# Eight modulation pages of layer 0 moved from between the projection pages into the feed-forward

## The chip, the cores and the metric

The kernel is one program on one core of one Trainium2 chip. The metric is device time in microseconds (us) of one execution, first as the median of several runs of the same kernel. The core has five engines that the text names: TensorE (PE: matmuls, and PEld its weight loads), VectorE (DVE), ScalarE (ACT), GpSimd (POOL) and SyncE (SP), which here only issues the transfers of weights. Sixteen DMA engines carry all transfers.

## What is computed

The reference is one inference step of a decoder with two layers, over 256 prompt tokens and 8 sample tokens (264 columns in the kernel), with a model width of 1024, all in float32. Cut to what matters here, a layer is:

```
mod = silu(c) @ w_ada_l + b_ada_l                 # 9 rows of c; w_ada_l is 1024 x 6144
sh1, sc1, gt1, sh2, sc2, gt2 = split(mod, 6)      # 1024 columns each
h = rms_norm(x, g_mix_l) * (1 + sc1) + sh1
q, k, v, u, g = in_proj(h, w_in_l, ...)           # 1024 x 4096
... attention, pooling, two branch projections, output projection ...
x = x + gt1 * (merged @ w_out_l)
h2 = rms_norm(x, g_ffn_l) * (1 + sc2) + sh2
f = swiglu(h2, ...)   in layer 0,   moe_swiglu(h2, ...)   in layer 1
x = x + gt2 * f
```

So `gt2`, the last sixth of the modulation, is needed only after the feed-forward of its layer.

## The kernel before

**Pages.** All weights of layer 0, and those of layer 1 up to its experts, are one list of pages, `stream`, written out by `layer_pages(l)`. A page is 512 KB and fills one of the 18 slots (`RING`) of the tile `ring`, page n in slot n % 18. SP walks through the list: before it loads page n it waits until page n - 18 is used (`s.pages_used`). TensorE takes the pages in the same order (`page()`) and waits for each one's arrival. Pages of the kinds in `PAIRED` come two in one transfer of 1 MB. Before the first page of `cache_v` SP reads sixteen table entries into registers. After the straight part of the list, layer 1's experts stream through the same slots and a few more.

**Modulation.** `w_ada` of a layer has 48 pages, eight for each sixth of `mod`; page n holds 128 input rows of one sixth. `modulation(l, n, b)` (L989) issues four weight loads of 32 columns and four matmuls of 256 columns for a page, and sums eight pages in one half of PSUM bank `b`. `read_mod` on DVE waits for the last page, transposes the bank (L1591) and adds the bias into `mod` (L1592). Layer 0's pages 0 to 15 come ahead of everything. Its pages 16 to 47 lie between the 32 projection pages: `later_ada(l, i)` puts four of them behind each odd projection page i from 1 to 15. Pages 32 to 47 sum into bank 1.

**Projection.** `z(i)` (L1080) is one projection page: eight matmuls of 128 x 264. Behind z(12) come the transposes of the samples' queries and keys (L1161, L1164). DVE copies them (`read_samples`, L1655 to L1661), POOL writes them to memory (`q_rows`, L685) and reads the first four back spread over all partitions (L687, 1 MB), and DVE starts the sample scores on them (`past_scores`, L1669 and L1672), two samples' worth before `comb_m` (L1793) and this layer's third `read_mod`. Meanwhile DVE forms the pooling input behind z(13) and z(14) (`window_sums`, L1687 to L1690, `pooled_minus_own`, L1697 to L1702). Behind z(17), TensorE transposes half of the values into bank 1 (`by_tokens`, L1085), and for that it waits until the third `read_mod` of the layer has read that bank (`s.mod_out`). Layer 1 has the same order, but in it no modulation page lies behind z(5), and its third `read_mod` reads eight pages instead of sixteen.

**Feed-forward of layer 0.** Before it TensorE works off sixteen modulation pages of layer 1 into bank 7 while the norm is computed. Then come four groups of hidden tiles, `FF_GROUPS = (6, 6, 5, 5)`. A group of n is n pairs of gate and up pages (`gate_up`, `column`, L981) and n down pages (`full_down`, L1277), which are freed only at the end of the group. DVE reads layer 1's modulation out of bank 7 when it begins group 1 (groups count from 0), and `add_f` uses `mod[40:48]` after the last group.

**Experts of layer 1.** 32 turns, each of gate and up pages (L1408) and down pages (L1428), some 11 MB a turn, one behind the other to the end.

Of the kernel before, what the change touches and what calls it, by code (L numbers as in the profile page):

```python
# [25 lines left out]
S = 256  # L26
# [26 lines left out]
FF_GROUPS = (6, 6, 5, 5)  # L53
# [83 lines left out]
def build(nc, A, O, const_in):  # L137
    ctx = ExitStack()
    with ctx:
        def sb(name, shape, dt=F32):  # L140
            return ctx.enter_context(nc.sbuf_tensor(name, shape, dt))

        def sem(name):
            return ctx.enter_context(nc.semaphore(name))
# [8 lines left out]
        sq = sb("sq", [P, DC, T])  # L153
# [128 lines left out]
        s = namedtuple("Semaphores", names)(*[sem(name) for name in names])  # L282
# [17 lines left out]
        def cols(w, j, n=1):  # L300

            return w[:, j * P:(j + n) * P].rearrange("(c p) n -> p c n", p=P)

        def ada_page(l, n):

            q, r = n // DC, n % DC
            return ("ada", l, n), A["w_ada"][l, r * P:(r + 1) * P, q * D:(q + 1) * D].rearrange("p (c n) -> p c n", c=DC)

        def later_ada(l, i):

            first, last = ((16, 48), (32, 40))[l]
            return range(first + 2 * (i - 1), min(first + 2 * (i + 1), last)) if i % 2 else range(0)

        def layer_pages(l):

            if l == 0:
                for n in range(16):
                    yield ada_page(l, n)
            else:
                for n in range(16, 32):  # L320
                    yield ada_page(l, n)
            for i in range(0, ZC + GC, 2):
                yield ("z", l, i), cols(A["w_in"][l], Z_ORDER[i], 2)
                yield ("z", l, i + 1), None
                for n in later_ada(l, i + 1):
                    yield ada_page(l, n)
                if i + 1 in V_AT:
                    for b in range(4):
                        yield ("v", l, 4 * V_AT.index(i + 1) + b), None
            for kind, w in (("branch", A["w_branch"]), ("out", A["w_out"])):  # L330
                for j in range(0, 8, 2):
                    yield (kind, l, j), cols(w[l], j, 2)
                    yield (kind, l, j + 1), None
            if l:
                for n in range(40, 48):
                    yield ada_page(l, n)
            if l == 0:
                for n in range(16):
                    yield ada_page(1, n)
                at = 0  # L340
                for n in FF_GROUPS:
                    for j in range(at, at + n):
                        yield ("gate", l, j), cols(A["w_ff_gate"][0], j)
                        yield ("up", l, j), cols(A["w_ff_up"][0], j)
                    for j in range(at, at + n):
                        yield ("down", l, j), A["w_ff_down"][0][j * P:(j + 1) * P, :].rearrange("p (c n) -> p c n", c=DC)
                    at += n

        stream = [page for l in range(LAYERS) for page in layer_pages(l)]
# [5 lines left out]
        for n, (key, _) in enumerate(stream):  # L355
            first = n - key[2] % 2 if key[0] in PAIRED else n
# [11 lines left out]
        def used_up(kind, l, i):  # L368

            return number[(kind, l, i)] + 1  # L370
# [591 lines left out]
        def _(pe):  # L962
            used = [0]

            def page(kind, l, i):

                n = used[0]
                assert stream[n][0] == (kind, l, i)
                at, count = arrives[n]
                pe.wait_ge(page_in[at], count)  # L970
                used[0] += 1
                if kind in PAIRED:
                    return pair_cols(at)[:, :, (i % 2) * P:(i % 2 + 1) * P]
                return slot(n % RING)
# [78 lines left out]
            for l in range(LAYERS):  # L1053
# [94 lines left out]
                for i in range(16):  # L1148
# [3 lines left out]
                    if 2 <= i < 10:  # L1152
                        j = i - 2
# [107 lines left out]
                def gate_up(c, k):  # L1261

                    for half, kind, read in ((0, "gate", s.silu_out), (1, "up", s.act_out)):
                        if c >= 2 or k:
                            pe.wait_ge(read, k + max(c - 1, 0))
                        column(bank[2 * half + c % 2][:, 0:T], page(kind, l, k + c), hT, 2 * DC * l + DC if k + c == 0 else None)

                def full_down(n, k, adds):

                    downs = [page("down", l, k + c) for c in range(n)]  # L1270
                    for j in range(DC):
                        if j >= 3 or adds:
                            pe.wait_ge(s.y_added, adds + max(j - 2, 0))
                        for c in range(n):
                            if j == 0:
                                pe.wait_ge(s.act_out, k + (c + 1))
                            mm = pe.matmul(bank[4 + j % 3][:, 0:T], downs[c][:, j, :], FFN["act"][:, c, :],  # L1277
                                           start=(c == 0), stop=(c == n - 1))
                            if j == DC - 1:
                                mm.then_inc(s.pages_used, 1)  # L1280
                        if j < DC - 1:
                            mm.then_inc(s.y_mm, 1)

                if l == 0:
                    k = 0
                    for i, n in enumerate(FF_GROUPS):
                        for c in range(n):
                            gate_up(c, k)
                        full_down(n, k, DC * i)
                        k += n  # L1290


# [173 lines left out]
            with pe.Else():  # L1466
# [8 lines left out]
                with pe.Fori(0, E) as e:  # L1475
                    with pe.Fori(0, BODIES) as b:
                        n = e * BODIES + b
                        for c in range(BODY):
                            if c >= 2:
                                pe.wait_ge(s.act_e, n * BODY + (c - 1))  # L1480
                            for r in range(DC):
                                at = eslot[2 * r]
# [13 lines left out]
                        for j in range(DC):  # L1496
                            if j >= 4:
                                pe.wait_ge(s.all_added, n * DC + (j - 3))
                            for i in range(BODY):
                                at = eslot[2 * DC + i]  # L1500
# [20 lines left out]
        def _(dve):  # L1521
            step = Step(dve, s.dve_step)
# [65 lines left out]
            def read_mod(l, b, first, last, spare, n=16):  # L1588
                at = S * (first // 8 % 2) if n == 8 else 0
                dve.wait_ge(s.pages_used, used_up("ada", l, last))  # L1590
                step(dve.transpose(spare, bank[b][:, at:at + 32 * n]))  # L1591
                return dve.tensor_tensor(mod[:, first:first + n, :], spare.rearrange("p (c n) -> p c n", c=n)[:, :, 0:NC],  # L1592
                                         vecT[:, 48 * l + first:48 * l + first + n].unsqueeze(2).broadcast_to([P, n, NC]),
                                         ALU.add)
# [10 lines left out]
            for l in range(LAYERS):  # L1605
# [159 lines left out]
                spare = ATT["prob"].rearrange("p a b -> p (a b)")[:, 0:512]  # L1765
# [22 lines left out]
                if l == 0:  # L1788
                    dve.wait_ge(s.lam_exp, 1)
                    for n in range(LAYERS):  # L1790
# [1 line left out]
                        step(dve.tensor_scalar(neglam[:, n:n + 1], neglam[:, n:n + 1], -LAM_INIT[n], None, ALU.add))  # L1792
                step(dve.scalar_tensor_tensor(out=comb_m[:, :], in0=const("comb_b", 64), scalar=neglam[0:64, l:l + 1],  # L1793
                                              in1=const("comb_a", 64), op0=ALU.mult, op1=ALU.add))
                if l:
                    read_mod(l, 1, 32, 39, spare[:, 0:S], 8).then_inc(s.mod_out, 1)
                else:
                    read_mod(l, 1, 32, 47, spare).then_inc(s.mod_out, 1)
                past_scores(2); read_v(0); past_scores(3); read_v(1); past_scores(4); past_scores(5); read_new()
                scores(0); past_scores(6); scores(1); weights(0); past_scores(7); scores(2); weights(1); scores(3); weights(2)  # L1800
                sample_top()
# [17 lines left out]
                for half in range(2):  # L1819
                    at = 520 * half  # L1820
# [53 lines left out]
                if l == 0:  # L1874
                    step(dve.memset(f, 0.0))
                    k = 0
                    for i, n in enumerate(FF_GROUPS):
                        if i == 1:
                            read_mod(1, 7, 0, 15, sq[:, :, :].rearrange("p a b -> p (a b)")[:, 0:512]).then_inc(s.mod_out, 1)
                        for c in range(n):  # L1880
                            dve.wait_ge(s.silu_out, k + c + 1)
                            dve.wait_ge(s.pages_used, used_up("up", 0, k + c))
                            dve.tensor_tensor(act_t[:, c, :], bank[2 + c % 2][:, 0:T], silu[:, c, :],  # L1883
                                              ALU.mult).then_inc(s.act_out, 1)
                        k += n
                        for j in range(DC):
                            if j < DC - 1:
                                dve.wait_ge(s.y_mm, (DC - 1) * i + j + 1)
                            else:
                                dve.wait_ge(s.pages_used, used_up("down", 0, k - 1))  # L1890
                            if i:
                                dve.wait_ge(s.y_added, DC * (i - 1) + j + 1)
                            dve.tensor_tensor(f[:, j, :], bank[4 + j % 3][:, 0:T], f[:, j, :], ALU.add).then_inc(s.y_added, 1)
                    dve.wait_ge(s.y_added, DC * len(FF_GROUPS))
                    add_f(f)
                else:
                    experts(dve, step, f, act_t, silu, add_f, read_mod)
# [26 lines left out]
```

## Time and profile before

| | us |
|---|---|
| median of 3 runs | 1658.96 |
| lowest and highest | 1658.45, 1659.12 |
| the profiled execution's own time | 1660.19 |
| its span, first to last instruction | 1658.5 |
| TensorE busy in the span | 1604.6 (97%) |
| DMA, mean of the span | 323 GB/s |

The rows further down are from that one profiled execution. "Busy" is the time in which an engine had an instruction in work; matmuls overlap, so neighbouring rows of TensorE overlap by some tenths of a microsecond. The text in square brackets at the end of a row of the timeline is the engine's idle time before that row and what ended it. Queue q1 is SP's, q0 is POOL's.

### The profile page before, as it was taken

What the parts mean: (1) busy time and instruction counts of PE and PEld (TensorE: products, weight loads), DVE (VectorE), ACT (ScalarE), POOL (GpSimd) and SP (SyncE); (2) the same over time, 40 slices, a digit from 0 to 9 for tenths busy, and PEclk for the clock granted to TensorE, in tenths of its full rate; (3) what the DMA queues carried; (4) which work ended last, traced back from release to release, by engine and by line L of the source; (5) the groups of instructions that cost most, each with busy time, mean ns of one, the idle gap of its engine ahead of it and who ended that gap; (6) DMA issues with size and microseconds to landing.
All of it is one profiled execution on the core that took longest, in us unless ns stands there. A gap on an engine that the chain in (4) does not pass through costs nothing.

```text
span 1658.5 us, 35090 instructions
## 1 busy us (share of the span) xinstructions
PE 1604.6 (97%) x15752; PEld 1016.4 (61%) x15752; DVE 423.6 (26%) x970; ACT 158.5 (10%) x410; POOL 67.3 (4%) x114
## 2 busy tenths in 40 slices
PE   6999999999999999999999999999999999999997
PEld 3778887888886888863444444654454535554444
DVE  3468353101103793542010101010101001010114
ACT  2102301000002113130000000000000000000000
POOL 3101300000000010001000000000000000000100
PEclk9999999999999999999999999999999999999999
DMA  9998868664448876439999999999999999999994
GB/s 346 386 375 301 308 214 257 162 203 147 133 140 305 269 256 216 137 134 376 402 410 399 409 409 400 408 407 398 405 395 406 404 393 402 408 390 407 409 399 187
DMA packets 225642, 535.43 MB, mean 323 GB/s; under 512 B 17069, under 2 KB 117083, under 8 KB 212690
## 3 DMA queue, kind: packets, MB, share of 16 engines
q1 hardware_dynamic: 210000, 497.11, 80.5%
q0 software_dynamic: 8608, 28.65, 4.7%
q10 hardware_dynamic: 6882, 7.38, 1.4%
q8 instruction: 127, 2.08, 0.5%
q14 instruction: 25, 0.20, 0.0%
HBM read 517.71 MB, written 15.82 MB: 322 GB/s over the span
## 4 chain that ended last, share of the span: by engine, by line
PE 79%; DMA 12%; DVE 4%; SPq 3%; issue 1%; ACT 0%; DVEq 0%
PE bank L1408 28%; PE bank L1428 14%; PE bank L1080 12%; PE bank L981 9%; PE bank L1277 5%; DMA ring<-in_w_exp_up 5%; DMA area<-in_w_exp_down 4%; PE bank L1253 3%; PE bank L1241 2%; PE bank L989 1%; DMA ring<-in_w_exp_gate 1%; SPq L598 1%; DMA ring<-in_w_ada 1%; DMA ring<-in_w_exp_down 1%; DVE inv L1834 1%
## 5 line engine op out<-in xcount | busy, mean ns | idle before, releaser
L1408 PE MATMUL bank<-ring,xT 128*32 128x448 f32 x3072 | 294.5, 539 | 8.3 <-issue 4.4
L1408 PE MATMUL bank<-ring,area 128*32 128x448 f32 x3072 | 293.2, 539 | 4.0 <-issue 3.2
L482 DVE TENSOR_TENSOR area<-bank,area 128x224 f32<-128x224 f32 x96 | 54.2, 565 | 783.0 <-ACT area L934 782.9
L1080 PE MATMUL bank<-hT,ring 128*128 128x264 f32 x1024 | 240.6, 391 | 2.9 <-ACT hT L778 2.9
L1408 PEld LDWEIGHTS bank<-ring,xT 128*32 128x32 f32 x3072 | 113.8, 110 | 180.9 <-issue 173.6
L1408 PEld LDWEIGHTS bank<-ring,area 128*32 128x32 f32 x3072 | 118.2, 110 | 170.9 <-issue 153.2
L1428 PE MATMUL bank<-area 128*32 128x256 f32 x3840 | 217.0, 379 | 2.3 <-DMA area<-in_w_exp_down 1.4
L1080 PEld LDWEIGHTS bank<-hT,ring 128*128 128x128 f32 x1024 | 194.3, 192 | 38.6 <-issue 6.2
L1428 PEld LDWEIGHTS bank<-area 128*32 128x32 f32 x3840 | 141.9, 110 | 70.5 <-DMA area<-in_w_exp_down 3.6
L981 PE MATMUL bank<-hT,ring 128*128 128x264 f32 x704 | 157.4, 386 | 0.0
L981 PEld LDWEIGHTS bank<-hT,ring 128*128 128x128 f32 x704 | 133.7, 190 | 23.2 <-issue 0.4
L934 ACT ACTIVATE area<-bank 128x224 f32<-128x224 f32 x96 | 34.3, 357 | 778.9 <-PE bank L1408 778.9
L1428 PE MATMUL bank<-ring,area 128*32 128x256 f32 x1536 | 90.7, 380 | 1.7 <-DMA ring<-in_w_exp_down 1.5
L1428 PEld LDWEIGHTS bank<-ring,area 128*32 128x32 f32 x1536 | 54.9, 110 | 42.0 <-issue 18.7
L1277 PE MATMUL bank<-area,ring 128*128 128x264 f32 x352 | 79.0, 386 | 0.0
L1277 PEld LDWEIGHTS bank<-area,ring 128*128 128x128 f32 x352 | 66.9, 190 | 11.4
L1253 PE MATMUL bank<-hT,ring 128*128 128x264 f32 x256 | 57.3, 386 | 0.0
L1253 PEld LDWEIGHTS bank<-hT,ring 128*128 128x128 f32 x256 | 48.6, 190 | 8.3
L989 PE MATMUL bank<-ring,cT 128*32 128x256 f32 x768 | 49.1, 398 | 2.2 <-DMA ring<-in_w_ada 1.6
L1883 DVE TENSOR_TENSOR area<-bank,area 128x264 f32<-128x264 f32 x22 | 9.5, 433 | 145.4 <-PE bank L981 145.4
L989 PEld LDWEIGHTS bank<-ring,cT 128*32 128x32 f32 x768 | 22.9, 113 | 24.2 <-issue 6.4
L727 POOL DMA_INDIRECT hT<-y_rows,row_of x2 | 1.9, 968 | 810.5 <-ACTq L950 810.2
(300 smaller groups left out, 880.4 us busy)
## 6 DMA issues: line engine op xcount, KB each, us to landing
ring<-in_w_exp_gate SPq DMA_DIRECT2D x256, 448.0 KB, 16.1
ring<-in_w_exp_up SPq DMA_DIRECT2D x256, 448.0 KB, 16.1
area<-in_w_exp_down SPq DMA_DIRECT2D x64, 1024.0 KB, 18.0
ring<-in_w_ada SPq DMA_DIRECT2D x96, 512.0 KB, 9.6
ring<-in_w_in SPq DMA_DIRECT2D x32, 1024.0 KB, 12.3
ring<-in_w_exp_down SPq DMA_DIRECT2D x32, 1024.0 KB, 15.6
area<-in_w_exp_down SPq DMA_DIRECT2D x32, 512.0 KB, 19.3
ring<-in_w_ff_gate SPq DMA_DIRECT2D x22, 512.0 KB, 6.8
```

The lines of the kernel that those rows point to most:

```text
L482: dve.tensor_tensor(F["act_tok"][:, t, :].rearrange("p (i n) -> p n i", i=BODY), bank[t][:, SLICE:2 * SLICE].rearrange("p (n i) -> p n i", ...
L598: sp.dma_start(wide(at)[:, 0:WIDE], w[0, e, r * P:(r + 1) * P, b * WIDE:(b + 1) * WIDE]).then_inc(page_in[at], 16)
L934: act.activation(FFN["silu_tok"][:, t, :], bank[t][:, 0:SLICE], ACT.Silu).then_inc(s.silu_e, 1)
L981: mm = pe.matmul(out, w[:, c, :], x[:, c, :], start=(c == 0), stop=(c == DC - 1))
L989: mm = pe.matmul(bank[b][32 * g:32 * g + 32, half * S:(half + 1) * S].rearrange("p (c n) -> p c n", c=DC), cT[:, r, :], w[:, :, 32 * g:32 ...
L1080: mm = pe.matmul(bank[b][:, 0:T], w[:, c, :], hT[:, c, :], start=(c == 0), stop=(c == DC - 1))
L1241: mm = pe.matmul(bank[4 + j % 2][:, 0:T], branch[j][:, c, :], oT[:, c, :], start=(c == 0), stop=(c == H - 1))
L1253: mm = pe.matmul(bank[out_bank[j % 3]][:, 0:T], w[:, c, :], hT[:, c, :], start=(c == 0), stop=(c == DC - 1))
L1277: mm = pe.matmul(bank[4 + j % 3][:, 0:T], downs[c][:, j, :], FFN["act"][:, c, :], start=(c == 0), stop=(c == n - 1))
L1408: mm = pe.matmul(bank[t][32 * g:32 * g + 32, 0:2 * SLICE].rearrange("p (s n) -> p s n", s=2), tokens[:, t, 32 * r:32 * r + 32], w[:, :, SL ...
L1428: mm = pe.matmul(bank[3 + t // 2][32 * q:32 * q + 32, (t % 2) * S:(t % 2 + 1) * S], FFN["actT"][:, m % 2, t, 32 * i:32 * i + 32], wide(at) ...
L1834: step(dve.reciprocal(inv[:, :], root[:, h % 2, :]))
```

## The change

Pages 40 to 47 of layer 0's modulation (`gt2`) leave their places behind z(13) and z(15). They come in the list behind the down pages of the feed-forward's second group, TensorE works them off there into bank 7, and DVE reads them when it begins the third group. Layer 0's third `read_mod` now reads eight pages, as layer 1's does. The wait for `s.mod_out` ahead of them makes sure that bank 7 has been read.

```diff
         def later_ada(l, i):

-            first, last = ((16, 48), (32, 40))[l]
+            first, last = ((16, 40), (32, 40))[l]
             return range(first + 2 * (i - 1), min(first + 2 * (i + 1), last)) if i % 2 else range(0)
...
                     for j in range(at, at + n):
                         yield ("down", l, j), A["w_ff_down"][0][j * P:(j + 1) * P, :].rearrange("p (c n) -> p c n", c=DC)
+                    if at == FF_GROUPS[0]:
+                        for j in range(40, 48):
+                            yield ada_page(0, j)
                     at += n
...
                         full_down(n, k, DC * i)
+                        if i == 1:
+                            pe.wait_ge(s.mod_out, 4)
+                            for j in range(40, 48):
+                                modulation(0, j, 7)
                         k += n
...
-                if l:
-                    read_mod(l, 1, 32, 39, spare[:, 0:S], 8).then_inc(s.mod_out, 1)
-                else:
-                    read_mod(l, 1, 32, 47, spare).then_inc(s.mod_out, 1)
+                read_mod(l, 1, 32, 39, spare[:, 0:S], 8).then_inc(s.mod_out, 1)
...
                     for i, n in enumerate(FF_GROUPS):
+                        if i == 2:
+                            step(read_mod(0, 7, 40, 47, sq[:, 0, 0:S], 8))
                         if i == 1:
                             read_mod(1, 7, 0, 15, sq[:, :, :].rearrange("p a b -> p (a b)")[:, 0:512]).then_inc(s.mod_out, 1)
```

## Rows read from the trace of the kernel before

**Rows 1.** The page: span and TensorE's total beside the other engines'.

```profile
span 1658.5 us, 35090 instructions
...
PE 1604.6 (97%) x15752; PEld 1016.4 (61%) x15752; DVE 423.6 (26%) x970; ACT 158.5 (10%) x410; POOL 67.3 (4%) x114
```

**Rows 2.** TensorE's timeline, layer 0, from the modulation pages behind z(13).

```profile
111.21 1.93 PE L989 MATMUL bank<-ring,cT 128*32 128x256 f32 x32
113.07 7.39 PE L1080 MATMUL bank<-hT,ring 128*128 128x264 f32 x32
120.39 1.93 PE L989 MATMUL bank<-ring,cT 128*32 128x256 f32 x32
...
130.68 0.55 PE L1085 MATMUL bank<-cst,area 128*128 128x128 f32 x3 [0.60 <-DVE mod L1592]
```

**Rows 3.** The chain that ended last, same stretch: start, length, what.

```profile
109.21 5.19 DMA q_rows<-area
...
114.69 8.00 DMA area<-q_rows
...
128.51 0.17 DVE neglam L1791
...
129.28 0.26 DVE comb_m L1793
...
129.56 0.73 DVE area L1591
```

**Rows 4.** DVE's timeline, layer 0, its copy of z(13).

```profile
111.38 0.43 DVE L1629 COPY area<-bank 128x264 f32<-128x264 f32 x1 [0.79 <-PE bank L1080]
```

**Rows 5.** The timeline of layer 1 at the same steps.

```profile
576.64 0.43 DVE L1629 COPY area<-bank 128x264 f32<-128x264 f32 x1 [0.78 <-PE bank L1080]
...
592.23 0.45 DVE L1591 STREAM_TRANSPOSE area<-bank 128x256 f32<-128x256 f32 x1
...
593.00 0.66 PE L1085 MATMUL bank<-cst,area 128*128 128x128 f32 x4 [1.78 <-DVE mod L1592]
```

**Rows 6.** DMA issues from 111 to 113 us: KB each, median us to landing.

```profile
ring<-in_w_in SPq DMA_DIRECT2D x2, 1024.0 KB, 12.4
```

**Rows 7.** DMA issues from 577 to 594 us, same columns.

```profile
area<-q_rows POOLq DMA_DIRECT2D x1, 1024.0 KB, 5.8
```

**Rows 8.** SP's timeline at the beginning of the feed-forward.

```profile
260.48 0.58 SPq L578 DMA_DIRECT2D ring<-in_w_ff_up  x1
263.20 0.37 SPq L578 DMA_DIRECT2D ring<-in_w_ff_gate  x1
```

**Rows 9.** TensorE's timeline there.

```profile
262.50 7.11 PE L989 MATMUL bank<-ring,cT 128*32 128x256 f32 x128
269.55 5.83 PE L981 MATMUL bank<-hT,ring 128*128 128x264 f32 x25
```

**Rows 10.** Windows: length, PE, PEld, DVE, ACT, POOL busy, granted clock, DMA share, GB/s.

```profile
111.00:122.00 11.00, 11.00 (x98) 7.87 (x96) 8.81 (x27) 0.00 (x0) 1.08 (x2) 1.00 1.08 364
131.00:180.00 49.00, 49.00 (x303) 42.19 (x301) 37.19 (x87) 12.53 (x44) 8.18 (x15) 1.00 0.75 259
...
397.90:433.50 35.60, 35.60 (x162) 30.40 (x161) 2.16 (x5) 1.95 (x5) 0.00 (x0) 1.00 0.72 212
...
990.00:1240.00 250.00, 244.06 (x3204) 128.69 (x3200) 24.52 (x60) 11.36 (x31) 0.00 (x0) 1.00 1.03 403
```

**Rows 11.** Windows in and behind a pause of TensorE at 40 us, same columns.

```profile
40.00:42.00 2.00, 0.59 (x2) 0.52 (x3) 1.96 (x6) 1.24 (x4) 0.00 (x0) 0.66 1.03 407
42.00:44.00 2.00, 2.00 (x6) 1.59 (x5) 2.00 (x6) 2.00 (x6) 0.00 (x0) 0.50 1.07 384
```

**Rows 12.** TensorE's timeline behind that pause, and behind a pause among the experts.

```profile
41.41 10.34 PE L1080 MATMUL bank<-hT,ring 128*128 128x264 f32 x32 [2.04 <-ACT hT L778]
...
1580.94 16.15 PE L1408 MATMUL bank<-ring,xT 128*32 128x448 f32 x168 [2.24 <-DMA ring<-in_w_exp_up]
```

**Rows 13.** The window at that second pause, columns as in rows 10.

```profile
1580.00:1584.00 4.00, 3.06 (x32) 1.15 (x36) 0.00 (x0) 0.00 (x0) 0.00 (x0) 1.00 1.03 402
```

## The prediction

> **What bounds the kernel now.** I read the page first. TensorE is busy for 97% of the span and no other engine for more than 26% [rows 1]. So whatever TensorE pays stands in the time, unless it pays it where it would otherwise have waited. The windows tell the stages apart [rows 10]. From 111 to 122 us and from 131 to 180 us TensorE has no idle time; in the feed-forward, 397.9 to 433.5 us, it is busy for 35.60 of 35.60 us with the DMA share at 0.72. In the experts both TensorE and the DMA engines are full: from 990 to 1240 us TensorE is busy for 244.06 of 250 us with the DMA share at 1.03, so the stream of pages ends the kernel there. That stream starts when layer 1 gives its slots free, so a delay ahead of the experts moves it by the same amount; the experts absorb nothing.
>
> Then I read TensorE's timeline and the chain of waits at the place that the pages leave [rows 2, 3]. The reader is to see that TensorE has almost no slack there, but something else runs just as long beside it: queries to memory (5.19 us), back over all partitions (8.00 us), sample scores on DVE, `read_mod`, and only then the value transposes at L1085. TensorE arrives there only 0.60 us too early [rows 2]. Two chains end nearly together, and the change shortens one of them.
>
> **What the pages free.** Two groups of four pages leave TensorE's queue between z(13) and L1085. Each holds it for 1.86 us (111.21 to 113.07 [rows 2]), together 3.72 us. The instruction behind z(17) has its release at 130.68 us whether TensorE comes early or not. So of the 3.72 us nothing is gained by itself; TensorE waits 0.60 + 3.72 = 4.32 us in place of 0.60, less what the other chain gets shorter.
>
> What gets shorter in that chain is `read_mod`. From the start of its transpose to L1085 layer 0 takes 130.68 - 129.56 = 1.12 us with sixteen pages [rows 2, 3], layer 1 takes 593.00 - 592.23 = 0.77 us with eight [rows 5]. That is 0.35 us. The bound from above is layer 1's whole stretch: from DVE's copy of z(13) to L1085 it takes 593.00 - 576.64 = 16.36 us with DVE never waiting, while layer 0 takes 130.68 - 111.38 = 19.30 us [rows 2, 4, 5]. Layer 0 has four small DVE instructions more for `neglam`, in the same chain; they stay, at 129.28 - 128.51 = 0.77 us [rows 3]. So at most 19.30 - 16.36 - 0.77 = 2.17 us come back, and only if the 1 MB transfer of the queries lands by the time that DVE has finished the pooling input. In layer 1 that transfer takes 5.8 us [rows 7] against 8.00 us in layer 0 [rows 3].
>
> I take 0.35 us, not 2.17. The transfer is slow in layer 0 because SP's queue is full beside it: DMA share 1.08 [rows 10]. A pair of projection pages issued right behind z(13) lands after 12.4 us [rows 6], near 123.7 us, after the queries at 122.69 us. So the pages already ordered by then keep the engines busy until the queries are in, and the pages that SP orders later, as the modulation pages are used up, stand behind them. The change removes only those later orders. Up to z(13) TensorE uses the pages at the same times, so SP orders as many bytes as before; eight of them are just other pages.
>
> The Trainium skill ("DMA: Bandwidth & Descriptors", "Queues, rings and completion order") says that a DMA engine takes turns between the queues that have work, packet by packet. By that rule a shorter line in SP's queue helps POOL's transfer only once the line is empty, which gives the sum that I take and not the 2.17 us.
>
> **What the pages cost where they go.** In the feed-forward nothing is idle beside which they could lie [rows 10]. Sixteen such pages before it take 269.55 - 262.50 = 7.05 us with the clock at full rate [rows 9], so eight take 3.52 us. By the small groups of rows 2 they would take 3.72 us, which is the upper bound; nothing excludes no part of it being hidden, and no row speaks for less. The place costs nothing more, for these reasons. DVE's added `read_mod` takes 0.77 us by layer 1's, while TensorE works on the first pair of the third group; DVE had only 2.16 us of work in 35.60 us [rows 10]. The wait for `s.mod_out` is for a read that DVE did at the beginning of the group that is just over. The issues of SP: eight pages move past some ninety others in its queue, but none is added. The ring: when full_down of the second group ends, 18 slots hold its six down pages, the eight modulation pages and four more, and the eight are used in 3.52 us. A harder case stands in the trace. Ahead of the feed-forward the sixteen modulation pages leave room for only two gate and up pages; SP's next order goes out at 263.20 us, after the first page is used [rows 8], and TensorE goes on into L981 without an idle row [rows 9]. If this cover failed, one page landing late would cost TensorE that lateness directly.
>
> **What is moved past.** Layer 0's list from z(14) to the second group is eight pages earlier in the ring, so SP reads its table entries, and loads values, branch and output pages, earlier than before. TensorE waited for no page in 131 to 180 us [rows 10], so that gains nothing. From L1085 on, DVE and TensorE start together as before, only 0.35 us earlier.
>
> **The sum.** Profiled execution 1660.19 us, minus 0.35, plus 3.52, is 1663.36 us. That execution lies 1.23 us above the median of the runs, so against the median it is 1658.96 + 3.17 = 1662.13 us. A measurement of this kernel tells differences from about 0.2%, here 3.3 us; the forecast, +0.19%, stands just inside it.
>
> **Rival 1: the clock falls in the new pause.** After the change TensorE waits 4.32 - 0.35 = 3.97 us before L1085. Against such a pause: behind 2.24 us of waiting among the experts the granted clock stays at 1.00, the level of 2.4 GHz [rows 12, 13]. For it: behind 2.04 us of waiting at 41 us it is 0.50, the level of 1.2 GHz [rows 11], and 32 matmuls of z take 10.34 us [rows 12] where the same 32 take 120.39 - 113.07 = 7.32 us or less at full clock [rows 2], some 3.0 us lost. That pause came behind thin work, this one behind dense work, but it is about twice as long as either. The price is 3.0 us. Its far end is 3.4 us: a mean clock of 0.66 from 40 to 42 us [rows 11] is half rate for 1.36 us of the 2, so the fall began 0.77 us before the matmul at 41.41 us, and that part, worth 0.4 us to a busy engine, cost nothing there. It all stands in the time, because 131 to 180 us has no idle time. It gives 1662.1 + 3.0 = 1665.1 us. It decides when the pause is long enough to pull the clock down at all; a pause of 0.60 us did not.
>
> The Trainium skill ("TensorE: Matmul & The Clock Gate", "HAM oscillation — how this bites in real kernels") describes a kernel whose waits of 3 to 5 us between bursts bring the clock down each time. By that rule this rival is what happens; no row here has such a wait behind dense work.
>
> **Rival 2: the queries land sooner**, and the full 2.17 us come back: 1658.96 + 3.52 - 2.17 = 1660.31 us, no measurable change. It needs the transfer to be slowed by the depth of SP's queue; the 5.8 us of layer 1 speak for it, the 12.4 us of rows 6 against it. The pause would be 2.15 us, and the clock would stay.
>
> **Rival 3: faster.** The 3.72 us taken out have to be a real saving: L1085 would have to be released by TensorE's own progress and not by DVE's. Then, with 0.60 us of waiting gone too, the pages' cost of 3.52 us is more than repaid, by up to 0.8 us. Only with a further saving, pages hidden in the feed-forward, does it get past 3.3 us: 1658.96 - 3.72 = 1655.2 us. The 0.60 us wait, ended by DVE [rows 2], and the windows without idle time [rows 10] both speak against it.
>
> **How the numbers follow.** Forecast (no fall of the clock) 0.46; rival 1, 0.40; rival 2, 0.09; rival 3, 0.03; a small loss from something unseen 0.02. The forecast's own range is 1661.4 to 1662.9 us: the sum, 0.2 us for the upper price of the pages and 0.5 us for the scatter of the runs. The bound of 0.2% is 1662.3 us and cuts it almost in half: 0.25 within, 0.21 slower. Slower in all is 0.21 + 0.40 + 0.02 = 0.63, within 0.2% it is 0.25 + 0.09 = 0.34, and faster 0.03. The range reaches from rival 2 (1660.31, less 0.2 of scatter) to rival 1 with 3.4 us and the upper price of the pages (1662.13 + 3.4 + 0.2, and 0.5 of scatter): 1660.1 to 1666.2 us.
>
> **What the profile after would show.** L1085 behind z(17) waits about 4 us for DVE's L1592, and starts near 130.3 us; the transfer of the queries still takes about 8 us (right) or 6 us (rival 2). The granted clock from 130 to 140 us is 1.00 (forecast) or 0.50 for part of it (rival 1). In the feed-forward a row of L989 with 64 matmuls stands for 3.5 us between L1277 and L981, with no idle time behind it. From there on everything is 3.2 us later than before, to the end. What would make me wrong: the clock; a page that comes late behind the eight; or experts whose stream doesn't shift with their start.

## The result, and the profile after

The changed kernel takes 1662.44 us (median of 17 runs, 1660.87 to 1663.75); the kernel before, run beside it, 1659.12 us (median of 17, 1657.44 to 1663.06). The ratio is 1.0019, with a 95% interval of 1.0013 to 1.0026: slower by 3.3 us, a small difference that the interval still sets apart from none. The profiled execution took 1663.29 us, with a span of 1661.5 us. The forecast was 1662.1 us. The profile shows that the sum came out right although several of its terms did not.

TensorE's timeline of the changed kernel, at the place that the pages left. It answers to [rows 2]; every line number behind the change is three to seven higher, so L1083 is z, L1088 the value transposes, L992 the modulation:

```profile
102.05 3.83 PE L1083 MATMUL bank<-hT,ring 128*128 128x264 f32 x16
...
106.59 14.41 PE L1083 MATMUL bank<-hT,ring 128*128 128x264 f32 x64
120.83 0.60 PE L1088 MATMUL bank<-cst,area 128*128 128x128 f32 x4
121.27 3.73 PE L1083 MATMUL bank<-hT,ring 128*128 128x264 f32 x16
127.55 1.11 PE L1088 MATMUL bank<-cst,area 128*128 128x128 f32 x4 [2.56 <-DVE mod L1599]
128.46 8.27 PE L1083 MATMUL bank<-hT,ring 128*128 128x264 f32 x32
136.56 0.60 PE L1180 MATMUL bank<-cst,area 128*8 128x128 f32 x4
```

z(13) to z(16) now run in one piece. The wait behind z(17) has grown, from 0.60 us, but to 2.56 us and not to the 3.97 us of the forecast. TensorE comes there 124.99 - 102.05 = 22.94 us (127.55 less the 2.56 us of waiting is 124.99) behind the start of z(12), where it was 130.08 - 103.01 = 27.07 us: it is 4.13 us earlier, not 3.72 us, and 0.60 + 4.13 less the 2.17 us found below is the 2.56 us. And the work behind it is slow: 1.11 us for four transposes that take 0.66 us in layer 1 [rows 5], 8.27 us for 32 matmuls that take 7.29 us elsewhere. The windows of the same execution tell why (columns as in [rows 10]):

```profile
125.00:126.00 1.00, 0.00 (x0) 0.00 (x0) 0.92 (x3) 0.39 (x1) 0.38 (x1) 1.00 1.02 375
...
127.00:128.00 1.00, 0.45 (x2) 0.46 (x3) 0.46 (x2) 0.00 (x0) 0.00 (x0) 0.51 1.03 410
...
129.00:130.00 1.00, 1.00 (x4) 0.79 (x3) 0.97 (x2) 0.00 (x0) 0.00 (x0) 0.50 1.05 389
130.00:131.00 1.00, 1.00 (x5) 0.79 (x4) 0.94 (x2) 0.00 (x0) 0.54 (x1) 0.78 1.02 363
131.00:132.00 1.00, 1.00 (x6) 0.87 (x5) 0.96 (x2) 0.00 (x0) 0.39 (x1) 1.00 1.09 354
```

Since 125.00 us TensorE has had nothing to do; near 127.0 us the granted clock goes from 1.00 to 0.50, that is from 2.4 to 1.2 GHz, and it is back near 130.4 us: the mean of 0.78 from 130 to 131 us is half rate for 0.44 us of it.

DVE's timeline tells why the wait is short. Before the change DVE had two waits of its own in this stretch, for z(14), which stood behind the modulation pages of z(13), and for the queries:

```profile
117.00 0.43 DVE L1629 COPY area<-bank 128x264 f32<-128x264 f32 x1 [0.49 <-PE bank L1080]
...
122.72 0.69 DVE L1669 TENSOR_TENSOR area<-area 128x512 f32<-128x512 f32 x1 [1.27 <-DMA area<-q_rows]
```

After it, with rows that answer to [rows 3 to 5]:

```profile
110.42 0.43 DVE L1636 COPY area<-bank 128x264 f32<-128x264 f32 x1 [0.79 <-PE bank L1083]
...
115.58 0.43 DVE L1636 COPY area<-bank 128x264 f32<-128x264 f32 x1
...
119.94 0.68 DVE L1676 TENSOR_TENSOR area<-area 128x512 f32<-128x512 f32 x1
...
126.78 0.45 DVE L1598 STREAM_TRANSPOSE area<-bank 128x256 f32<-128x256 f32 x1
...
128.83 0.69 DVE L1676 TENSOR_TENSOR area<-area 128x512 f32<-128x512 f32 x1 [1.34 <-DMA area<-in_cache_k]
```

The sample scores start at 119.94 us with no wait for the queries (the wait in the last row, for cached keys, comes back below). From DVE's copy of z(13) to L1088 it is 127.55 - 110.42 = 17.13 us, where it was 19.30 us: the whole 2.17 us that the prediction gave only as the upper bound. It has three parts. From the copy of z(13) to that of z(14) it is 5.16 us in place of 5.62 us, 0.46 us less. From there to the first sample score it is 4.36 us in place of 5.72 us, 1.36 us less. And from the transpose of `read_mod` to L1088 it is 0.77 us in place of 1.12 us, 0.35 us less. The DMA issues from 113 to 122 us say the same of the transfer, 4.9 us in place of 8.00 us in [rows 3]:

```profile
area<-q_rows POOLq DMA_DIRECT2D x1, 1024.0 KB, 4.9
```

In the feed-forward the timeline of TensorE answers to [rows 9]:

```profile
374.72 21.52 PE L1280 MATMUL bank<-area,ring 128*128 128x264 f32 x96
396.17 3.66 PE L992 MATMUL bank<-ring,cT 128*32 128x256 f32 x64
399.76 35.87 PE L984 MATMUL bank<-hT,ring 128*128 128x264 f32 x160
```

No idle time on either side. To lay two executions beside each other I measure distances on TensorE: from the start of z(12) to the first modulation page ahead of the feed-forward (the attention stretch), from there to the first modulation page behind the feed-forward (the feed-forward stretch), and from there to the first matmul of the experts (the rest of layer 1). The start of z(12) differs between the executions, by some 2 us: it lies at 102.29 to 104.01 us in three with the pages in their old place and at 101.64 to 103.07 us in ten without them. I count none of it for the change, and that is not shown.

| | attention stretch, us | feed-forward stretch, us | rest of layer 1, us |
|---|---|---|---|
| before (103.01, 262.50, 504.71, 744.53) | 159.49 | 242.21 | 239.82 |
| after (102.05, 260.77, 506.76, 746.94) | 158.72 | 245.99 | 240.18 |
| difference | -0.77 | +3.78 | +0.36 |

The sum is +3.37 us. The medians differ by 3.32 us, with an interval of 2.2 to 4.3 us. The -0.77 us is the release 2.17 us sooner, less the 1.40 us that the work from L1088 to L1180 takes longer (136.56 - 127.55 = 9.01 us in place of 138.29 - 130.68 = 7.61 us); behind that work the stretch is as long as before.

The +0.36 us stands nearly whole in one wait of TensorE for DVE, at the norm ahead of layer 1's feed-forward, before and then after:

```profile
723.56 0.71 PE L1020 MATMUL bank<-sq,cst 128*128 128x264 f32 x2 [1.43 <-DVE sq L1864]
```

```profile
725.96 0.71 PE L1023 MATMUL bank<-sq,cst 128*128 128x264 f32 x2 [1.76 <-DVE sq L1868]
```

It is small and it is no scatter. The wait is 1.76 us in the changed kernel and in every kernel derived from it below, without the pages too, and this stretch takes 240.14 to 240.18 us in them (240.78 us in after_reads_early); the wait is 1.39 to 1.43 us and the stretch 239.79 to 239.83 us in the kernel before and in those derived from it. No run tells its cause.

### The profile page after: what moved, and what is told of

The parts are those of the page before. It is cut to its first block, busy times and chain, and to the rows that moved or that the text cites. A ratio compares the mean times of both kernels' runs of the same rounds, so it can differ in the third digit from the quotient of the medians.

```text
span 1661.5 us, 35093 instructions
## 1 busy us (share of the span) xinstructions
PE 1605.6 (97%) x15752; PEld 1021.3 (61%) x15752; DVE 423.8 (26%) x972; ACT 158.4 (10%) x410; POOL 67.3 (4%) x114
## 4 chain that ended last, share of the span: by engine, by line
PE 81%; DMA 11%; DVE 5%; SPq 2%; issue 1%; ACT 0%; DVEq 0%
PE bank L1415 29%; PE bank L1435 14%; PE bank L1083 12%; PE bank L984 9%; DMA ring<-in_w_exp_up 6%; PE bank L1280 5%; PE bank L1256 3%; DMA area<-in_w_exp_down 2%; PE bank L1244 2%; PE bank L992 2%; DMA ring<-in_w_exp_gate 1%; DMA ring<-in_w_ada 1%; DVE inv L1838 1%; SPq L581 1%; PE bank L1231 1%
## 5 line engine op out<-in xcount | busy, mean ns | idle before, releaser
L1083 PE MATMUL bank<-hT,ring 128*128 128x264 f32 x1024 | 239.7, 390 | 2.9 <-ACT hT L781 2.9
L1083 PEld LDWEIGHTS bank<-hT,ring 128*128 128x128 f32 x1024 | 194.3, 192 | 37.8 <-issue 5.4
L992 PE MATMUL bank<-ring,cT 128*32 128x256 f32 x768 | 49.1, 400 | 2.1 <-DMA ring<-in_w_ada 1.5
L992 PEld LDWEIGHTS bank<-ring,cT 128*32 128x32 f32 x768 | 23.0, 113 | 23.9 <-issue 6.1
```

Source lines behind the costliest of these rows:

```text
L992: mm = pe.matmul(bank[b][32 * g:32 * g + 32, half * S:(half + 1) * S].rearrange("p (c n) -> p c n", c=DC), cT[:, r, :], w[:, :, 32 * g:32 ...
L1083: mm = pe.matmul(bank[b][:, 0:T], w[:, c, :], hT[:, c, :], start=(c == 0), stop=(c == DC - 1))
```

## Why the queries landed sooner: SP's register reads

The prediction held that SP's orders keep the DMA engines full until the queries are in. SP's timeline shows what it overlooked. Before, it orders six pairs of projection pages up to 119 us and then nothing until 130 us:

```profile
101.25 18.00 SPq L573 DMA_DIRECT2D ring<-in_w_in  x6
130.07 1.95 SPq L584 DMA_DIRECT2D ring<-in_cache_v  x4
```

After:

```profile
95.29 11.76 SPq L576 DMA_DIRECT2D ring<-in_w_in  x4
116.82 4.53 SPq L587 DMA_DIRECT2D ring<-in_cache_v  x8
```

The gap of some ten microseconds is the sixteen table entries that SP reads into registers ahead of its first page of `cache_v`. The view of that line, before and then after (durations of one in ns, minimum, median and maximum, then first and last start in us):

```profile
L582 SPq TENSOR_LOAD <-table x16: 261/266/469, 120.5 to 129.4; - x16
```

```profile
L585 SPq TENSOR_LOAD <-table x16: 261/266/470, 107.2 to 116.1; - x16
```

From the first start to the last it is 8.9 us for fifteen, 0.6 us apiece with what follows each. The Trainium skill ("DMA: Bandwidth & Descriptors", "Latency and other measured facts") gives about 600 ns as the floor of a `tensor_load`; the 0.6 us from one start to the next agree with it, while the record of one load lasts only 0.27 us. The list after z(13) is eight pages shorter, so the slot of SP's first `cache_v` page is free once z(11) and three of the modulation pages behind it are used, not only when z(15) is; SP comes to it at 107 us, when its orders ahead of it are out. For ten microseconds it orders nothing and its queue runs dry: the DMA share from 114 to 115 us is 0.81 where it was 1.08, and from 116 to 117 us not one packet of SP's queue moves, where in the kernel before 346 do. The transfer of the queries lies just there. Behind its order it moved nothing at first in either kernel: for about 1 us now (ordered at 113.54 us), and for 3.8 us or more before (ordered at 114.69 us), while SP's queue alone filled the engines.

**Run before_reads_107.** The kernel before, with the reads put where the change had put them:

```diff
             for n, (key, src) in enumerate(stream):
+                if key == ("z", 0, 22):
+                    sp.wait_ge(s.inputs_in, INPUTS)
+                    cached = [sp.value_load(table[0:1, i:i + 1], min_val=0, max_val=PHYS - 1) for i in range(NS * PAGES)]
                 if key[0] in PAIRED:
```

> The kernel before, with only SP's sixteen register reads moved: ahead of its order for z(22), so that they fall near 107 to 117 us, where they fall in the changed kernel, instead of near 120 to 130 us. Theory (the reads stop SP's orders, its queue runs dry and the 1 MB transfer of the queries has the DMA engines to itself): the transfer takes about 5 us instead of 8.00, the 0.60 us wait at L1085 goes, and the kernel gets 0.6 us faster, ratio 0.9996. Rival (it is the missing modulation pages that made the transfer fast in the changed kernel): the transfer stays at about 8 us, the wait at 0.60 us, the ratio at 1.0000.

The transfer took 5.6 us and the wait at L1088 was gone (DMA issues, then TensorE's timeline):

```profile
area<-q_rows POOLq DMA_DIRECT2D x1, 1024.0 KB, 5.6
```

```profile
129.19 0.60 PE L1088 MATMUL bank<-cst,area 128*128 128x128 f32 x4
...
138.47 0.62 PE L1185 MATMUL bank<-cst,area 128*23 128x128 f32 x4 [1.11 <-DVE area L1685]
```

So the place of the reads alone makes the transfer fast; the missing modulation pages are not needed for it. On DVE's side the reads give 1.36 of the 2.17 us: from its copy of z(13) to the transpose of `read_mod` it is 127.48 - 110.66 = 16.82 us, where the kernel before has 18.18 us and the changed one 16.36 us. The wait of 0.50 us for z(14) is still there, for it is the pages that make it. But the 0.6 us that were expected of it did not come: 1658.86 us, ratio 0.9999 (0.9990 to 1.0008), and the attention stretch of 160.23 us is 0.74 us longer than before. The time saved at L1088 is lost again at L1185, which waits for DVE, and DVE waits 2.78 us for a transfer of cached keys. Those keys come later too: 131.32 - 102.29 = 29.03 us behind the start of z(12), where it was 27.92 us before.

```profile
131.32 0.69 DVE L1672 TENSOR_TENSOR area<-area 128x512 f32<-128x512 f32 x1 [2.78 <-DMA area<-in_cache_k]
```

**Run after_reads_early.** The changed kernel with the same three lines at `("z", 0, 8)`, near 50 us.

> The changed kernel, with only SP's register reads moved: ahead of its order for z(8), near 50 us, so that SP orders without a break from 100 to 120 us. Theory of the reads: the queries' transfer takes about 8 us again as before, L1088 waits about 4.5 us instead of 2.56, and the kernel is 2 us slower than the changed one, about 1.0031 of the kernel before, and up to 1.0040 where the clock falls for longer. Rival (missing pages): the transfer stays at 4.9 us, the wait at 2.56 us, and the ratio at 1.0019.

The transfer took 7.9 us again and the wait at L1091 (the same transposes) was 4.11 us:

```profile
129.30 1.11 PE L1091 MATMUL bank<-cst,area 128*128 128x128 f32 x4 [4.11 <-DVE mod L1602]
130.21 9.63 PE L1086 MATMUL bank<-hT,ring 128*128 128x264 f32 x32
```

This is the pause that the prediction forecast, and the clock did not survive it: six windows of 1 us from 129 to 135 us show 0.50 to 0.53, and the 32 matmuls take 9.63 us. The attention stretch is 161.63 us, and the kernel takes 1666.35 us, ratio 1.0041 (1.0028 to 1.0055). Against the changed kernel the attention stretch is 2.91 us longer: 1.55 us of it is the longer pause and 1.36 us the work from L1091 to L1183 at the lower clock. Had SP's reads not moved, the change would have cost twice what it did.

**Run before_reads_early.** The kernel before with the reads at `("z", 0, 8)`, to see whether that place costs anything of its own.

> The kernel before, with SP's register reads ahead of its order for z(8), near 50 us, as in the run of the changed kernel with early reads. It tells whether reads at that place cost anything of their own. Theory: no; the queries' transfer stays at 8 us, the wait at 0.60 us, ratio 1.0000 within 0.0004. Rival (a page ordered late near 60 us makes TensorE wait, and this was part of the 1.0041 of the other run): a wait for a page between 50 and 100 us, ratio 1.001 or more.

It took 1659.65 us, ratio 1.0001 (0.9992 to 1.0010), transfer 7.9 us, wait 0.40 us, stretch 159.35 us. The place costs nothing that can be told, and the 1.0041 is the pause, the clock and what the pages cost in the feed-forward.

## What the clock's fall cost

**Run after_filler.** Matmuls with no use keep TensorE at work in the pause:

```diff
+                        if l == 0 and i == 17:
+                            pe.wait_ge(s.ks_ready, 1)
+                            for c in range(11):
+                                pe.matmul(bank[7][:, 0:T], ident, hT[:, c % DC, :], start=True, stop=True)
                         pe.wait_ge(s.mod_out, 3 * l + i - 14)
```

> The changed kernel, with eleven extra matmuls of 128 x 264 into a free part of bank 7 ahead of the wait at L1088 of layer 0 (2.4 us of work in a pause of 2.56 us; their result is not used). Theory (the pause brings the clock down for the work behind it): the granted clock stays at 1.00 from 125 to 135 us, and the kernel is 1.4 us faster than the changed one, about 1.0011 of the kernel before. Rival (the clock falls at some fixed time or the loss is of another cause): the clock row shows 0.50 all the same and the ratio stays at 1.0019.

I mis-sized it. A matmul in fp32 stands as two instructions, so these are 22 of 0.225 us and last past the pause:

```profile
125.42 5.06 PE L1178 MATMUL bank<-hT,cst 128*128 128x264 f32 x22
130.32 0.60 PE L1088 MATMUL bank<-cst,area 128*128 128x128 f32 x4
130.75 7.29 PE L1083 MATMUL bank<-hT,ring 128*128 128x264 f32 x32
```

The clock stayed at 1.00 and the work behind ran at full speed (7.29 us), but the kernel took 1663.34 us, ratio 1.0027 (1.0017 to 1.0038), since TensorE came over 2 us too late.

**Run after_filler_short.** `range(5)` in place of `range(11)`.

> The changed kernel with five extra matmuls ahead of the wait at L1088 of layer 0, not eleven: the run with eleven showed that each is two instructions of 0.225 us, so that they took 4.9 us and ran 2.3 us past the pause. Five are 2.25 us in a pause of 2.56 us. Theory: the granted clock stays at 1.00, L1088 starts when DVE releases it, and the kernel gets back the 1.4 us that the clock cost, ratio about 1.0011 against the kernel before. Rival (the loss behind the pause is not of the clock): the clock is 1.00 and the work from L1088 to L1180 still takes 9.0 us in place of 7.6, ratio 1.0019.

```profile
124.80 2.39 PE L1178 MATMUL bank<-hT,cst 128*128 128x264 f32 x10
127.50 0.66 PE L1088 MATMUL bank<-cst,area 128*128 128x128 f32 x4 [0.32 <-DVE mod L1603]
127.99 7.29 PE L1083 MATMUL bank<-hT,ring 128*128 128x264 f32 x32
135.12 0.60 PE L1184 MATMUL bank<-cst,area 128*8 128x128 f32 x4
136.35 0.62 PE L1189 MATMUL bank<-cst,area 128*23 128x128 f32 x4 [0.64 <-DVE area L1693]
```

The mechanism is as expected: with the pause filled the clock stays, and from L1088 to the next transposes it is 135.12 - 127.50 = 7.62 us, not 136.56 - 127.55 = 9.01 us. So the fall costs TensorE 1.4 us. But the kernel gets back less than that, and less than was expected: behind it there is now a wait for DVE of 0.64 us, at the same step as in before_reads_107, and the attention stretch is 158.20 us, only 0.5 us shorter than the changed kernel's. The time is 1661.72 us, ratio 1.0018 (1.0009 to 1.0027). It does not differ measurably from the changed kernel's 1.0019; the 0.5 us stands in the traces alone.

**Run after_again.** The changed kernel once more.

> The changed kernel once more, to see how far the fall of the clock differs between executions. Theory: the pause is 2.56 us again within 0.1 and the queries' transfer 5 us; the fall lasts 3 to 4 us and costs 1.4 to 1.8 us. Rival: in some executions there is no fall, and the work from L1088 to L1180 takes 7.6 us.

Transfer 5.0 us, pause 2.54 us, the same 1.11 us at L1088 and 8.38 us in place of 8.27 us; stretches 158.82 and 245.99 us, time 1661.32 us. All six profiled executions with a pause of 2.5 us or more in this place showed the fall; in three of those with 2.5 us (after_no_pages, after_one_matmul and after_no_matmul, below) it began only 0.7 to 0.9 us after TensorE was back at work, near 129 us, and there the 32 matmuls took 8.97 us, so that the fall cost 1.7 us. The two in which the pause was filled showed none.

## What the pages cost in the feed-forward

**Run after_no_pages.** Neither loads nor matmuls; gt2 of layer 0 is made from layer 1's modulation.

```diff
-                    if at == FF_GROUPS[0]:
-                        for j in range(40, 48):
-                            yield ada_page(0, j)
...
-                        if i == 1:
-                            pe.wait_ge(s.mod_out, 4)
-                            for j in range(40, 48):
-                                modulation(0, j, 7)
```

> The changed kernel with the eight pages left out of the feed-forward, loads and matmuls both; DVE reads layer 1's modulation in their place, so gt2 of layer 0 is not computed. Theory (in the feed-forward the pages cost their whole TensorE time): 3.5 us less than the changed kernel, so about 0.2 us less than the kernel before, ratio 0.9998. Rival (part of the loss is elsewhere, in transfers or in the experts' stream): the ratio stays above 1.0005.

1657.76 us, ratio 0.9994 (0.9985 to 1.0003); stretches 159.01 and 242.21 us. The feed-forward is back to the hundredth of a microsecond, so the pages' price there is 245.99 - 242.21 = 3.78 us. The rest of layer 1 stays at 240.18 us: the 0.36 us are not the pages'.

**Run after_one_matmul.** Pages loaded and waited for, one matmul a page in place of four:

```diff
-                                modulation(0, j, 7)
+                                w = page("ada", 0, j)
+                                pe.matmul(bank[7][0:32, S:2 * S].rearrange("p (c n) -> p c n", c=DC), cT[:, j - 40, :],
+                                          w[:, :, 0:32], start=(j == 40), stop=(j == 47),
+                                          skip_group_check=True).then_inc(s.pages_used, 1)
```

> The changed kernel with one matmul in place of four, and without the last half of what fp32 issues for them, for each of the eight pages in the feed-forward: all eight are still loaded, waited for and freed, but gt2 of layer 0 is not computed. Theory (what the pages cost there is TensorE's work): eight times two instructions of 0.055 us are 0.9 us in place of 3.5, so the kernel is 2.6 to 2.9 us faster than the changed one, ratio 1.0002 to 1.0004. Rival (part is the loads or the waits for them): the ratio stays above 1.0010.

This gave no answer: 1662.89 us, ratio 1.0022 (1.0013 to 1.0031), feed-forward stretch 245.97 us. The timeline shows why:

```profile
397.48 3.64 PE L1297 MATMUL bank<-ring,cT 128*32 128x256 f32 x16
401.05 35.87 PE L984 MATMUL bank<-hT,ring 128*128 128x264 f32 x160
```

Sixteen instructions take 3.64 us, and sixty-four take 3.66 us. The four matmuls of a page stand in four column groups of 32 and run side by side; leaving three out saves nothing. What a page costs is two instructions of 0.2275 us, however many of the four column groups have one.

**Run after_no_matmul.** Pages loaded and waited for, no matmul. TensorE's sequencer frees them, for which it waits until the down pages are done:

```diff
-                                modulation(0, j, 7)
+                                if j == 40:
+                                    pe.wait_ge(s.pages_used, used_up("down", 0, 11))
+                                page("ada", 0, j)
+                                pe.sem_inc(s.pages_used, 1)
```

> The changed kernel with no matmul at all for the eight pages in the feed-forward. They are still loaded and waited for, and TensorE's sequencer frees them, once the down pages of the group are done; gt2 of layer 0 is not computed. The run with one matmul a page gave no answer, since its sixteen instructions took 3.64 us, as long as the sixty-four. Theory (the cost there is TensorE's work and nothing of the loads): 3 to 3.8 us faster than the changed kernel, ratio 0.9996 to 1.0001. Rival (the loads or the waits for them cost): the ratio stays above 1.0010, with a wait for a page or a longer L984 behind them.

1660.37 us, ratio 1.0001 (0.9992 to 1.0010): the gain over the changed kernel is 2.1 us, less than the 3 to 3.8 us expected. The feed-forward stretch is 505.38 - 261.60 = 243.78 us: 2.21 us shorter than the changed kernel's, and 1.57 us longer than without pages. The row behind the place says what 1.34 us of that are:

```profile
398.41 35.84 PE L984 MATMUL bank<-hT,ring 128*128 128x264 f32 x160 [1.34 <-issue]
```

The profile puts it down to no page. I take it for the drain which the experiment itself puts in, the wait for the down pages; no run parts the two. Then the loads cost at most the 0.2 us that are left, and the price is TensorE's work.

## The pages in the pause instead

If a pause behind z(17) pulls the clock down, the pages can be the work that fills it. This run keeps them out of the projection's first half and out of the feed-forward:

```diff
+                if l == 0 and i == 16:
+                    for n in range(40, 48):
+                        yield ada_page(0, n)
...
+                    if l == 0 and i == 17:
+                        pe.wait_ge(s.ks_ready, 1)
+                        for n in range(40, 48):
+                            modulation(0, n, 7)
...
+                if l == 0:
+                    read_mod(0, 7, 40, 47, spare[:, 0:S], 8).then_inc(s.last_mod, 1)
+                    dve.wait_ge(s.last_mod, 1)
```

> The eight pages stand neither behind z(13) and z(15) nor in the feed-forward, but behind z(17), ahead of the wait at L1088, in bank 7, read by DVE ahead of the first scores. Theory: the pause of 2.56 us takes up that much of their 3.5 us, the clock stays at 1.00, nothing is added in the feed-forward, and L1088 starts about 1 us later than in the changed kernel; against the kernel before the stretch to the feed-forward is 0.5 to 1 us shorter, ratio 0.9994 to 0.9997. Rival (DVE, which waits for the cached keys, is the bound behind L1088, and 0.7 us more work on it takes the rest): the stretch is as long as before, ratio 1.0000 within 0.0003.

```profile
124.51 3.66 PE L992 MATMUL bank<-ring,cT 128*32 128x256 f32 x64
128.89 0.66 PE L1088 MATMUL bank<-cst,area 128*128 128x128 f32 x4 [0.72 <-DVE mod L1601]
129.38 7.29 PE L1083 MATMUL bank<-hT,ring 128*128 128x264 f32 x32
```

1657.93 us, ratio 0.9994 (0.9985 to 1.0003), stretches 158.86 and 242.20 us. SP's list is as long ahead of `cache_v` as before the change, so the queries take 7.9 us again, and the place still needs no more than 0.72 us of waiting. L1088 starts 1.75 us later behind z(12) than in the changed kernel (27.25 and 25.50 us), where about 1 us was expected. I ran it once more, since the interval held 1.

> The kernel with the eight pages behind z(17) once more, since its first interval, 0.9985 to 1.0003, did not settle whether it is faster than the kernel before. Theory: the stretch to the feed-forward is 0.6 us shorter, so the ratio is near 0.9996. Rival (the first ratio was scatter): 1.0000, with a stretch as long as before.

1659.52 us, ratio 1.0001 (0.9992 to 1.0010), wait 0.97 us, stretches 261.01 - 101.89 = 159.12 us and 503.22 - 261.01 = 242.21 us. The stretch is 0.4 to 0.6 us shorter than before in the traces, and the times do not tell this kernel from the kernel before. Beside the changed kernel it saves the 3.8 us of the feed-forward and the 0.36 us behind it and gives back 0.1 to 0.4 us of attention. It is no proven gain over the kernel before.

## Why the prediction was right, point by point

**That TensorE gains nothing by itself from the pages it no longer has there: right.** L1088 was released by DVE before and after. The 3.72 us were 4.13 us, which only made the pause longer. But z(14) came sooner to DVE, and of that 0.46 us reached the release; the prediction did not see DVE's wait of 0.49 us for z(14).

**"I take 0.35 us, not 2.17": wrong.** The release came the full 2.17 us sooner: 0.35 us by `read_mod`, as forecast, 1.36 us by the queries and 0.46 us by z(14). The failed step is the sentence that the pages already ordered keep the engines busy until the queries are in, with its ground that SP orders as many bytes as before up to z(13). The part on what is moved past had named SP's table reads, and said that their being earlier gains nothing. They are ten microseconds in which SP orders nothing, and the change moved them to 107 to 117 us, so that the engines ran out of SP's pages before the queries were in, near 118.4 us; before_reads_107 and after_reads_early show it from both sides.

**That the clock stays: wrong.** The pause was 2.56 us, shorter than the forecast 3.97, and the clock fell all the same, behind over 70 us of dense work. Rival 1 had the mechanism right, and a size for a longer pause: 3.0 us against 1.4 us here. The pause for which it was priced came about in after_reads_early, and there 32 matmuls took 2.3 us more and the transposes 0.45 us. All of the 1.4 us stands in the attention stretch; but filling the pause gives back only some 0.5 us of it, because DVE's wait for cached keys is the next bound.

**Rival 2** had the release right to the hundredth, and the clock and the pause wrong (2.15 us, for it too counted 3.72 us). The condition that it named, the depth of SP's queue, was not varied by any run; what the runs varied is when SP stops ordering.

**The cost in the feed-forward: 3.52 forecast, 3.78 measured.** The pages themselves took 399.76 - 396.17 = 3.59 us. The rest lies at the edges: the gate and up columns behind them took 435.47 - 399.76 = 35.71 us, where they took 433.41 - 397.81 = 35.60 us before, and the down part ahead of them 21.45 us in place of 21.36 us. Sixteen pages in one row [rows 9] hide such edges.

**That nothing else changes up to the experts: not quite.** The rest of layer 1 took 0.36 us more, a term that the prediction did not have and whose cause is open.

**That the experts pass the delay on: right, within what can be told.** At the start of the experts' first turn the changed kernel was 746.94 - 744.53 = 2.4 us later, at the end of the span 3.0 us. The experts took 0.6 us longer than before in this execution and 1.2 us less in after_again, so that much is scatter.

**The sum** was -0.35 + 3.52 = +3.17 us; the stretches give -0.77 + 3.78 + 0.36 = +3.37 us. Two errors of the attention stretch, a release 1.8 us sooner than forecast and a clock at half rate for some 3.4 us, took most of each other away. The 1662.1 us owed its closeness to that, and that was luck.

## What to carry to other kernels

Work taken out from ahead of a wait for another engine shortens little and makes a pause; ask what that pause does to the clock, and price the work at its new place by TensorE's bare streaming time, with no cover. When entries of a hand-written list of transfers move, everything in the issuing queue moves with them, also what is no transfer: ten microseconds of register reads decided here when another queue had the DMA engines to itself. And a saving ahead of two chains of nearly the same length is worth only the distance to the next one: behind this place the cached keys let 0.5 of 1.4 us through in after_filler_short and nothing of 0.6 us in before_reads_107.

## What the runs showed of the hardware that I had not expected

- Behind dense work, the clock went to 1.2 GHz in a pause of 2.54 to 2.56 us or within 0.9 us behind it, for about 3.4 us, in all five profiled executions that had it, while a wait of 1.78 us in layer 1 [rows 5] and one of 2.24 us among the experts [rows 12, 13] left it at 2.4 GHz. With 4.11 us of pause it stayed low for more than 6 us.
- Four fp32 matmuls of 32 columns in four column groups take as long as one alone: 64 instructions in 3.66 us, 16 in 3.64 us.
- The 1 MB of queries on POOL's queue landed 7.9 to 8.0 us after their order where SP went on ordering, and 4.9 to 5.6 us after it where SP had stopped and its queue ran dry. Before the change the difference is a wait ahead of the first packet: 3.8 us or more in which only SP's queue moved, 0.35 MB a microsecond. From 119 to 120 us the two queues then moved nearly as many packets, 42 of POOL's and 45 of SP's, but 0.34 MB and 0.04 MB. What ends the wait ahead of the first packet is not shown.
